# Two attention-value units by Strassen block products on TensorE and VectorE, and a position table laid out without a flip

## The reference

```
h = rms_norm(x, g_pre_mix) * (1 + sc_m) + sh_m      # sc_m, sh_m: parts of silu(c) @ w_ada, 2048 x 12288
proj = h @ w_in                                     # 256 x 2048 by 2048 x 7184
qa, ka, va, qb, kb, vb, rb, zb = split(proj)        # va: 1024 columns, 8 heads of 128
s = qa . ka / 8 + rel_bias[t5_bucket(kpos - qpos)]  # 8 heads, 2 maps each, masked by chunks of 64
pd = softmax(s[map 0]) - lam * softmax(s[map 1])
oa = rms_norm(pd @ va) ...                          # attention; beside it gated linear attention ob
y = concat([oa, ob]) @ w_out
x = x + gt_m * rms_norm(y)
```

## Time and profile before

| | |
|---|---|
| median of 3 runs | 1491.66 us (1490.12 to 1493.62) |
| the profiled execution | 1489.82 us, of which the span 1488.0 us |
| PE busy in the span | 1233.9 us, 83% |
| DVE busy | 754.2 us, 51% |
| ACT busy | 207.7 us, 14% |
| DMA | 581.93 MB, mean 391 GB/s |
| mean granted TensorE clock | 0.937 of full speed |

### The profile page before, as it was taken

The page is one execution under the profiler, slowest core; times in us unless marked ns, Lnnn a source line. Parts: engine busy times, 40 slices in busy tenths (PEclk is TensorE's granted clock), DMA queues, the critical chain, the costliest instruction groups (busy, mean ns, idle before and its releaser), DMA issues.

```text
span 1488.0 us, 18997 instructions
## 1 busy us (share of the span) xinstructions
PE 1233.9 (83%) x7349; PEld 544.5 (37%) x7350; DVE 754.2 (51%) x1090; ACT 207.7 (14%) x475; POOL 46.3 (3%) x68
## 2 busy tenths in 40 slices
PE   4699999999999999876777777676776779999976
PEld 4578644744444443321222222222221223333322
DVE  5876257777765866442243224323332335555525
ACT  3011131222101041100000000000000001111103
POOL 1000200000100020000000000000000000000010
PEclk9899999999999999999799788989988889999989
DMA  9999979888899689999999999999999999999996
GB/s 355 392 383 385 359 270 361 326 337 300 321 403 392 257 345 393 425 425 426 427 424 427 426 427 424 428 426 427 424 428 425 426 425 428 426 426 425 428 426 263
DMA packets 101668, 581.93 MB, mean 391 GB/s; under 512 B 6680, under 2 KB 31536, under 8 KB 57856
## 3 DMA queue, kind: packets, MB, share of 16 engines
q1 hardware_dynamic: 98752, 572.81, 94.7%
q10 hardware_dynamic: 1664, 6.46, 1.1%
q0 software_dynamic: 1216, 2.17, 0.6%
HBM read 579.29 MB, written 2.13 MB: 391 GB/s over the span
## 4 chain that ended last, share of the span: by engine, by line
PE 38%; DMA 36%; SPq 17%; DVE 6%; issue 1%; ACT 1%; POOL 0%; ACTq 0%; DVEq 0%
DMA stream<-in_w 32%; PE ps L710 11%; PE ps L923 6%; SPq L547 5%; SPq L566 5%; PE ps L635 4%; SPq L541 4%; PE ps L796 4%; PE ps L977 3%; DMA stream<-in_w_ada 3%; SPq L482 2%; PE ps L884 2%; PE ps L829 1%; PE ps L707 1%; DVE wk L1063 1%
## 5 line engine op out<-in xcount | busy, mean ns | idle before, releaser
L923 PE MATMUL ps<-stream,wk 128*32 128x512 f32 x2304 | 321.8, 686 | 134.1 <-DMA stream<-in_w 133.3
L1386 DVE TENSOR_TENSOR acc<-ps,acc 128x2048 f32<-128x2048 f32 x37 | 84.8, 2292 | 429.3 <-PE ps L884 429.3
L923 PEld LDWEIGHTS ps<-stream,wk 128*32 128x32 f32 x2304 | 70.8, 118 | 373.9 <-issue 297.0
L977 PE MATMUL ps<-stream,cst 128*32 128x512 f32 x1152 | 153.4, 661 | 61.9 <-DMA stream<-in_w 61.8
L710 PE MATMUL ps<-stream 128*128 128x512 f32 x448 | 197.0, 594 | 0.3 <-PE ps L635 0.3
L710 PEld LDWEIGHTS ps<-stream 128*128 128x128 f32 x448 | 83.4, 190 | 99.5 <-issue 98.8
L635 PE MATMUL ps<-stream 128*128 128x256 f32 x512 | 116.7, 391 | 1.8 <-ACT stream L1531 1.8
L635 PEld LDWEIGHTS ps<-stream 128*128 128x128 f32 x512 | 99.9, 196 | 16.4 <-issue 1.9
L930 PEld LDWEIGHTS ps<-cst,wk 128*128 128x128 f32 x576 | 70.1, 192 | 62.8 <-issue 62.8
L1063 DVE SCALAR_TENSOR_TENSOR wk<-stream,cc,wk 128x768 f32<-128x768 f32 (+1 forms) x90 | 83.6, 929 | 11.4 <-DMA stream<-in_w_ada 8.6
L884 PE MATMUL ps<-wk,cst 32*128 32x512 f32 x592 | 88.0, 665 | 0.8 <-ACT wk L1695 0.8
(11 more groups left out here) (273 smaller groups left out, 972.0 us busy)
## 6 DMA issues: line engine op xcount, KB each, us to landing
stream<-in_w SPq DMA_DIRECT2D x190, 2048.0 KB, 40.9
stream<-in_w_ada SPq DMA_DIRECT2D x64, 1024.0 KB, 7.0
stream<-in_w_in SPq DMA_DIRECT2D x8, 4096.0 KB, 16.4
stream<-in_w_ada SPq DMA_DIRECT2D x64, 384.0 KB, 10.0
stream<-in_w_out SPq DMA_DIRECT2D x4, 4096.0 KB, 17.0
stream<-in_w_ada SPq DMA_DIRECT2D x16, 512.0 KB, 9.9
stream<-in_w_in SPq DMA_DIRECT2D x4, 2048.0 KB, 13.7
stream<-in_w_in SPq DMA_DIRECT2D x2, 3072.0 KB, 16.3
```

The lines of the kernel that those rows point to most:

```text
L923: last = nc.tensor.matmul(bank(1 + m)[32 * g:32 * g + 32, :], xe[:, k + g, :], w13[m][:, k + g, :], start=(k == 0), stop=(k == KD - 4))
L977: last = nc.tensor.matmul(bank(2)[32 * g:32 * g + 32, :], hid[:, k, :], w2v[:, k, 512 * g:512 * g + 512], start=(k == 0), stop=(k == 3))
L1386: V.tensor_tensor(y4, ps[:, b0:b0 + 4, :], y4, ALU.add).then_inc(ysum_sb, 1)
```

## The change

Units 4 and 5 (both halves of va) are no longer filled by 64 matmuls of 512 columns each, but as 2x2 blocks: rows in two blocks of 128, k in two halves of 1024, columns in two halves of 256. Seven products of 8 k-blocks with 256 columns (`block_product`, two in each of a unit's first three slots and one in the fourth) take the place of eight. Their sums are on VectorE: four of the blocks of h once (`h_sum`, 128x1024 each), four of the blocks of w_in for each unit (`w_sum`, 128x2048, in place in the unit's buffer), eight of the outputs for each unit (`o_sum`, 128x256). Two products of a unit are copied out by ScalarE. The products use three PSUM banks in turn, so a product waits for the sums that read the bank before. The row item gives 128 partitions instead of 8 (row p is head p mod 8), reldram holds each row 128 times (1024 rows of 384), and the read back steps so that the table comes out in order; the flip item is gone. Slices of w_ada start one slot later (ADA_AT), and "row" moves from slot 1 to slot 0.

```diff
-ADA_AT = [0, 10, 20, 30, SLOTS + 3]
+BLOCK_UNITS = [4, 5]
+FILLS = HELD + SLOTS // 2 - 2 * len(BLOCK_UNITS)
+ADA_AT = [1, 11, 20, 30, SLOTS + 3]
...
-    beside[0].append(("alpha", 0))
-    beside[1].append(("row",))
+    beside[0] += [("alpha", 0), ("row",)]
-    beside[5].append(("flip",))
...
+        def block_bank(b, n):
+            return bank((0, 1, 6)[(7 * b + n) % 3])[:, 0:256]
+        hsum = [view(s3, 2048 + 1024 * i, 8, P) for i in range(4)]
-        reldram = dram("reldram", [A_HEADS, SKEW])
+        reldram = dram("reldram", [A_HEADS, P, SKEW])
...
@@ SyncE, unit loads
+                    elif i - 2 < len(BLOCK_UNITS):
+                        sp.wait_ge(blk_ps, 7 * (i - 1))
...
@@ TensorE
+                    if part == 0:
+                        pe.wait_ge(unit_in[b], 16)
+                        if b:
+                            pe.wait_ge(blk_out, 8 * b - 4)
+                        block_product(h_block(0, 0), quarter(b, 0, 0), 0)
+                        pe.wait_ge(blk_t, 3)
+                        if b:
+                            pe.wait_ge(blk_out, 8 * b - 1)
+                        block_product(hsum[2], quarter(b, 1, 1), 1)
+                    elif part == 1:
+                        if b:
+                            pe.wait_ge(blk_out, 8 * b)
+                        block_product(h_block(0, 1), quarter(b, 1, 0), 2)
+                        pe.wait_ge(blk_t, 4 * b + 6)
+                        block_product(hsum[3], quarter(b, 0, 1), 3)
+                    elif part == 2:
+                        pe.wait_ge(blk_t, 4 * b + 7)
+                        block_product(hsum[1], quarter(b, 1, 1), 4)
+                        pe.wait_ge(blk_out, 8 * b + 1)
+                        block_product(hsum[0], quarter(b, 0, 0), 5)
+                    else:
+                        pe.wait_ge(blk_t, 4 * b + 8)
+                        pe.wait_ge(blk_out, 8 * b + 2)
+                        block_product(h_block(1, 1), quarter(b, 1, 0), 6)
...
@@ VectorE
+            dve.wait_ge(hT_act, KD)
+            dve.wait_ge(stage_ps, len(STAGES) - 1)
+            h_sum(hsum[0], h_block(1, 0), h_block(1, 1), 1)
+            h_sum(hsum[1], hsum[0], h_block(0, 0), 2, ALU.subtract)
+            dve.wait_ge(stage_ps, len(STAGES))
+            h_sum(hsum[2], h_block(0, 1), hsum[1], 3, ALU.subtract)
+            h_sum(hsum[3], h_block(0, 0), h_block(1, 0), 4, ALU.subtract)
+                if part == 0:
+                    dve.wait_ge(unit_in[b], 16)
+                    dve.wait_ge(blk_ps, 7 * b + 1)
+                    w_sum(quarter(b, 0, 0), quarter(b, 0, 1), quarter(b, 0, 0), 4 * b + 5)
+                    w_sum(quarter(b, 0, 1), quarter(b, 1, 1), quarter(b, 0, 1), 4 * b + 6)
+                elif part == 1:
+                    dve.wait_ge(blk_ps, 7 * b + 2)
+                    w_sum(quarter(b, 1, 1), quarter(b, 1, 1), quarter(b, 0, 0), 4 * b + 7)
+                    dve.wait_ge(blk_ps, 7 * b + 3)
+                    o_sum(c11, c12, block_bank(b, 2), 8 * b + 1)
+                    w_sum(quarter(b, 1, 0), quarter(b, 1, 0), quarter(b, 1, 1), 4 * b + 8)
+                elif part == 2:
+                    dve.wait_ge(blk_ps, 7 * b + 4)
+                    o_sum(c21, c12, block_bank(b, 3), 8 * b + 2)
+                    dve.wait_ge(blk_ps, 7 * b + 5)
+                    o_sum(c12, c12, block_bank(b, 4), 8 * b + 3)
+                    o_sum(c21, c21, block_bank(b, 4), 8 * b + 4)
+                else:
+                    dve.wait_ge(blk_ps, 7 * b + 6)
+                    o_sum(c12, c12, block_bank(b, 5), 8 * b + 5)
+                    o_sum(c12, c12, c22, 8 * b + 6)
+                    o_sum(c22, c21, block_bank(b, 5), 8 * b + 7)
+                    dve.wait_ge(blk_ps, 7 * b + 7)
+                    o_sum(c21, c21, block_bank(b, 6), 8 * b + 8)
...
@@ GpSimd
-            pool.dma_start(reldram[:, :], relrow).then_inc(rel_out, 16)
+            pool.dma_start(reldram.rearrange("c q s -> q c s"), relrow.unsqueeze(1).to_broadcast((P, A_HEADS, SKEW))).then_inc(rel_out, 16)
-            pool.wait_ge(flip_sb, 4)
+            pool.wait_ge(bias_in, 16)
```

More of the change, by code:

```diff
@@ L61 @@
 ATT = 2 * A_HEADS
-HEADS_READY = [8, 10]
+HEADS_READY = [8, 16]
 FIN_DVE = [(0, 0), (0, 1), (1, 0), (1, 1), (1, 2)]
@@ L176, in schedule @@
     for s in range(SLOTS):
-        out.append(("proj",) + slot_unit(s))
+        i, half, part = slot_unit(s)
+        out.append(("block", i - 4, 2 * half + part) if i in BLOCK_UNITS else ("proj", i, half, part))
         out += beside[s]
@@ L391, in build @@
         proj_ps, proj_sb = sem("proj_ps"), sem("proj_sb")
+        blk_ps, blk_copy, blk_t, blk_out = sem("blk_ps"), sem("blk_copy"), sem("blk_t"), sem("blk_out")
         s_ps, s_sb, p_max, p_exp, pd_sb = sem("s_ps"), sem("s_sb"), sem("p_max"), sem("p_exp"), sem("pd_sb")
@@ L666, in _ @@
                 elif kind == "row":
-                    nc.tensor.matmul(bank(4)[0:A_HEADS, 0:SKEW], relb, bkt[:, 0:SKEW], start=True, stop=True).then_inc(relrow_ps, 1)
+                    nc.tensor.matmul(bank(4)[:, 0:SKEW], relb, bkt[:, 0:SKEW], start=True, stop=True).then_inc(relrow_ps, 1)
                 elif kind == "alpha":
@@ L702, in _ @@
                         pe.wait_ge(unit_in[i % 2], 16 * ((i - 4) // 2 + 1))
-                    if part == 0:
-                        pe.wait_ge(proj_sb, fill - 1 if fill > HELD + 1 else fill - HELD + 1)
+                    if part == 0 and fill > HELD + 1:
+                        pe.wait_ge(proj_sb, fill - 1)
+                    elif part == 0:
+                        pe.wait_ge(blk_out, 8 * len(BLOCK_UNITS) - 1 + fill - HELD)
                     if c in TRANSPOSED:
@@ L724, in _ @@
                             pe.wait_ge(s_sb, i)
-                        pe.wait_ge(proj_sb, HEADS_READY[h // 4])
+                        pe.wait_ge(proj_sb, HELD)
+                        pe.wait_ge(blk_out, HEADS_READY[h // 4])
                         for m in range(2):
@@ L1101, in _, with h_sum @@
                 added(len(STAGES) - 1, u)
+            def h_sum(out_, in0, in1, n, op=ALU.add):
+                V.tensor_tensor(out_, in0, in1, op).then_inc(blk_t, 1)
+                dve.wait_ge(blk_t, n)
+            dve.wait_ge(hT_act, KD)
[4 more added lines that the diff above has]
+            h_sum(hsum[2], h_block(0, 1), hsum[1], 3, ALU.subtract)
@@ new lines, in _, with w_sum, o_sum, block @@
+            h_sum(hsum[3], h_block(0, 0), h_block(1, 0), 4, ALU.subtract)
+            def w_sum(out_, in0, in1, n):
+                V.tensor_tensor(out_, in0, in1, ALU.subtract).then_inc(blk_t, 1)
+                dve.wait_ge(blk_t, n)
+            def o_sum(out_, in0, in1, n):
+                V.tensor_tensor(out_, in0, in1, ALU.add).then_inc(blk_out, 1)
+                dve.wait_ge(blk_out, n)
+            def block(b, part):
+                c11, c12, c21, c22 = [out_block(b, t, n) for t in range(TT) for n in range(2)]
+                if part == 0:
[7 more added lines that the diff above has]
+                    dve.wait_ge(blk_ps, 7 * b + 3)
+                    dve.wait_ge(blk_copy, 2 * b + 1)
+                    o_sum(c11, c12, block_bank(b, 2), 8 * b + 1)
[6 more added lines that the diff above has]
+                    o_sum(c21, c21, block_bank(b, 4), 8 * b + 4)
+                else:
+                    dve.wait_ge(blk_ps, 7 * b + 6)
+                    dve.wait_ge(blk_copy, 2 * b + 2)
+                    o_sum(c12, c12, block_bank(b, 5), 8 * b + 5)
[3 more added lines that the diff above has]
+                    o_sum(c21, c21, block_bank(b, 6), 8 * b + 8)
@@ L1189, in _ @@
                     accumulate(item[1])
+                elif kind == "block":
+                    block(item[1], item[2])
                 elif kind == "wout":
@@ L1554, in _ @@
                     act.wait_ge(relrow_ps, 1)
-                    A(relrow, bank(4)[0:A_HEADS, 0:SKEW], ACT.Copy).then_inc(relrow_sb, 1)
+                    A(relrow, bank(4)[:, 0:SKEW], ACT.Copy).then_inc(relrow_sb, 1)
                 elif kind == "lam":
@@ L1573, in _ @@
                         A(st[:, 32:48], bank(7)[:, 0:16], ACT.Exp, scale=1.0 / GATE_TAU).then_inc(suf_exp, 1)
-                elif kind == "flip":
-                    for j in range(4):
-                        act.wait_ge(flip_ps, j + 1)
-                        A(wk[:, 512 * j:512 * j + 512], bank((2, 3, 6)[j % 3]), ACT.Copy).then_inc(flip_sb, 1)
+                elif kind == "block":
+                    _, b, part = item
+                    if part == 0:
+                        if b == 0:
+                            act.wait_ge(stage_ps, len(STAGES))
+                        for n, out_ in ((0, out_block(b, 0, 1)), (1, out_block(b, 1, 1))):
+                            act.wait_ge(blk_ps, 7 * b + n + 1)
+                            A(out_, block_bank(b, n), ACT.Copy).then_inc(blk_copy, 1)
                 elif kind == "proj":
```

34 lines of the change are left out of this document (21 added, 13 removed).

## The result

The changed kernel takes 1499.79 us (median of 5 runs, 1497.49 to 1500.23), the kernel before 1491.66 (1490.12 to 1493.62, also 5 runs) beside it. The ratio is 1.0047 with a 95% interval of 1.0036 to 1.0058: 7 to 8 us **slower** (the interval is 5.4 to 8.7 us), where 5.9 us were forecast. The profiled execution took 1497.76 us, its span is 1495.8 (before: 1488.0).

What follows compares the result with a forecast made beforehand. No one engine bounds the whole kernel; VectorE, full from 199 us to step 15, decides: 231.1 + 133.9 + 6.5 - 4.1 + 0.4 = 367.8, 5.9 us late. Median 1491.66 + 5.9 = 1497.6 us, range 1494 to 1502.

Steps and rivals of the forecast that it cites:

- the working along VectorE's order: Following VectorE's work in order from slot 0 through attention step 15, which it would end 5.9 us later.
- the new wait: Near 197 us TensorE stands idle 8.4 us for unit 4's sums, queued on VectorE behind alpha 1, lam and two slices.
- the softmax of step 0: VectorE, without idle time from 199.25, reaches attention step 0 at 231.1 instead of 228.05 us.
- the slot at 368.70: The TensorE slot starting at 362.37 before, held by step 15's softmax, would start near 368.3.
- Rival D: Narrow records cost more: a block product takes 6.5 us, all later work 18 us later, about 1515 us; chance 0.02.
- C: Rival: slices come late behind unit loads, 2 to 4 us each place, 1503 us; chance 0.12.
- A: Rival: sums fit VectorE's idle time, TensorE keeps its 10.4 us, 1481.3 us; chance 0.12.
- the clock's fall behind the long wait: After the 8.4 us wait TensorE's half clock costs some 3 us, of which at most 0.5 shows.
- no wait gives anything back: From about 368 us on, TensorE's lateness of 5.9 us goes through to the end undiminished.
- the flip's 3.4 us: Dropping the flip was counted as part of TensorE's 10.4 us less work, beside 7.0 from the products.
- the sums that pace slot 6: Products of slots 4 and 5 run ahead of these VectorE sums, covering the clock's 3 us but for at most 0.5.
- four fifths of its gain are gone: TensorE's idle 8.4 us near 197 was said to use up most of its 10.4 us gain.

Runs made afterwards that it cites:

- after: The changed kernel as it is, first profile and measurement: 1499.79 us, 1.0047 of the kernel before.
- after_again: The changed kernel as it is, measured a second time: 1498.91 us, 1.0048 of the kernel before.
- sums_first: The changed kernel with unit 4's output sums 5 to 7 moved ahead of alpha 1 on VectorE: 1500.10 us, 1.0054 of the kernel before.
- short_sums: The changed kernel with unit 5's four weight sums cut to one of eight k-blocks: 1499.11 us, 1.0052 of the kernel before.
- both_less: The changed kernel with unit 4's last three sums ahead of alpha 1 and unit 5's weight sums cut to an eighth: 1499.49 us, 1.0045 of before.
- units_alone: The changed kernel with the old position table and its flip kept: 1502.94 us, 1.0073 of the kernel before.
- keep_clock: The changed kernel with idle matmuls in two TensorE waits, at attention step 6 and before the second output projection half: 1498.39 us, 1.0040 of before.
- slices_later: The changed kernel with w_ada slices spread over later slots (ADA_AT 1, 12, 22, 31): 1492.66 us, 1.0002 of the kernel before.
- one_unit: The kernel before with the new table, unit 2's load earlier, block products for unit 4 alone, its sums ahead of alpha 1: 1487.73 us, 0.9966.
- before_again: The kernel before, unchanged, measured and profiled a second time: 1492.99 us, 1.0008.

## Why the prediction was right, and where it wasn't

**The step that held best** is the working along VectorE's order. Alpha 1 at 189.21 (forecast 189.2); the new wait 8.57 us (8.4); no idle time from 199.22; the softmax of step 0 at 231.51 (231.1); the slot at 368.70 (368.3); between them VectorE waits for TensorE once, for 0.9 us (0.4). The prices: a w_sum is 2.29 us and two follow at 2.32 (2.33 taken), an o_sum 0.42, a block product 3.5. Rival D is dead with that: 256 columns cost half of 512. The Trainium skill (TensorE: Matmul & The Clock Gate, Back-to-back issue gap) gives about 81 ns for a matmul of 128 columns and 131 for one of 512 in a sustained stream, by which the narrow ones would be dear; this trace differs (0.22 us a record of 256 columns, 0.44 of 512), and the measurement decides. C didn't come, since the slice was in time; A didn't, since the wait was 8.6 and not under 3. The stretch from 368 to 439 passed the lateness on one for one, 70.9 us both times.

**The sizes.** Of the forecast 5.9 us, step 0 took 0.4 more, the 0.49 us at 225.69. I had said that of the clock's fall behind the long wait at most 0.5 would show: the fall took 2.6 us of TensorE's time and 0.49 came through. Up to the slot at 368.70 it is +6.3 against the first profile of before; against the second it is +5.6, so part of the close agreement is which profile stood beside it. The median is 2.2 us over the forecast; in the profiles 1.8 of this is the fall at 459 to 463, **a term that the sum lacked**. I had taken "no wait gives anything back" for "nothing is added" behind 368 us. TensorE waits 1.32 and 1.80 us there in both kernels (before at 435.62 and 452.46), and the clock fell in both profiles of after and in neither of before. Why there, no run settles: among all variants, those with two units by block products had it near 460 (after, after_again, sums_first, short_sums, both_less, units_alone), unless the wait was filled (keep_clock) or the slices moved (slices_later, where it came at 496); those with one unit or none had no fall at that place.

**The reason was too simple**, though its numbers were right. The prediction says that TensorE is ahead of VectorE from slot 6 on, by 227 or 227.6 against 231.1, and that the flip's 3.4 us are simply part of TensorE's gain. It compared the wrong events. VectorE works in order, and its sums of unit 5's product 4 stand two slices before the softmax, at 225.7, and there TensorE had no lead at all. So TensorE's work was on the path after all: with the flip kept, the change would have cost 3.5 us more (units_alone). The cover for the clock's fall, "the sums that pace slot 6", was there and was counted rightly, but the fall used it up: 2.6 us of fall and 0.49 of wait in after, 2.8 and 0.71 in after_again, 3.0 and 0.89 in keep_clock leave 2.1 us of cover each time. So it is the fall that made the two chains level; with a full clock behind the long wait TensorE would have been 2.1 us ahead there (an estimate from these three). Nor does "four fifths of its gain are gone" with the wait follow: without the wait the gain is gone just the same, in waits for weight sums and a second fall of the clock (sums_first). What sets step 0 are three chains, VectorE's work, the products with the fall, and unit 2's load, with 0, 0 and about 1.4 us of slack. Each of the first two was shown by shortening it alone and both together, the third by what stopped both_less. That is shown at step 0; how much of the whole time each chain takes is not, since the clock's falls differ by several us between the runs. That all three short give the time back is in one_unit, which changes other things too.

## What to carry to other kernels

Where work moves between engines that walk one list in order, compare the engines at every hand-over, not at the end of the stage: a slack of 0 at one sum in the middle makes both engines critical, and then an edit on either side alone gives nothing while a loss on either side counts in full. When an edit that takes work away gives nothing, look in the trace for the wait that grew, shorten that chain too, and expect a third. Add up the clock's falls in both profiles before a time is read as a verdict on a chain: here they differed by more than the edits gave. Before tuning the new work, move what can wait: here one list of slice positions was worth as much as the whole loss, and the change on one unit, with that list, an earlier load and earlier sums, 0.5%.

## What the hardware showed that I had not expected

The granted clock falls to half behind short waits too: behind 1.80 us (353.5 us in before_again) as behind 8.57. Behind a short one a fall mostly cost 1.4 to 1.7 us of TensorE's time, but 2.8 to 3.0 in four runs at 359 to 366 us, behind waits of 1.0 to 1.2 and then 1.8. Behind one of 1.21 it was 1.4 in both_less and 3.1 in sums_first. Behind the 8.6 it was 1.4 (short_sums) to 3.0 (keep_clock), behind 5.0, 1.7 and 0.9 in a row 3.2. The same wait doesn't always bring it (1.80 us at 352.76 in the first profile of before, with the clock at 1.00 from 353 to 359). In the attention part these falls come and go between executions; the two profiles of before differ by 1.6 us at the output projection with them.

The start of the slots, which no edit here touches but for two sums, lay anywhere from 163.8 to 166.7 us, so stages had to be compared from there and not from zero.

The 128-fold write of the table: GpSimd waited 10.95 us for it in after, 4.54 for the plain one before, so 6.4 us more where its bytes at the mean rate had suggested 4. Over the other runs the wait lay anywhere from 7.7 (slices_later) to 14.1 us (one_unit), and at 4.5 for the plain one each time. The read back was issued at 186.90 all the same, since the write starts 7 us or so earlier ("row" in slot 0). It had landed by 194.45, long before step 0, and no engine on the path waits for it.
